# Hybrid attention block, 1 core: the first keys and queries of the differential stage loaded during linear attention, and the output projection's operand split one step ahead of its product

## The chip, the core and the metric

The kernel runs on one core of one Trainium2 chip. TensorE (PE) multiplies, VectorE (DVE), ScalarE (ACT) and GpSimd (POOL) do the elementwise work, SyncE (SP) issues most transfers. The metric is device microseconds of a whole execution, as the median of several runs; the kernel before took 4082.74 us (3 runs, 4078.76 to 4084.45).

## The reference, cut to what matters

Two layers (DEPTH 2) of a transformer block on 1024 latent and 256 context tokens of width 1024, in float32. Each layer projects the normalized tokens to heads, runs three kinds of attention, joins them, projects them out and adds a SwiGLU part:

```
pl = project_heads(modulate(h_lat, ...) @ w_in[layer], ...)
gla_lat = gla_output(ol_f + ol_b, pl['go'], gla_norm_g[layer])            # gated linear attention
diff_lat = diff_output(diff_latent(pl['dq'], dk_all, dv_all, lam), ...)   # p0 - lam * p1 over all 1280 keys
swa_lat = swa_output(swa_latent(...))                                     # sliding window
y_lat = jnp.concatenate([gla_lat, diff_lat, swa_lat], axis=-1) @ w_out[layer]
h_lat_mid = post_norm(h_lat, y_lat, m_lat[2], ln_g[layer, 0], ln_b[layer, 0])
```

In layer 0 the context tokens go through the same steps; in layer 1 (the last) only the latent tokens are queries. Tokens lie in tiles of 128: 10 tiles in layer 0, 8 in layer 1.

## The kernel before

The stages run one after the other, each in a block of its own: every engine has its list of instructions, engines meet through semaphores, and a stage ends with a barrier of all engines and a clearing of its semaphores by POOL (`cleanup_on_exit`). A layer is: input norm and projection, `gated_linear_attention` (L756), `differential_attention` (L1767), `sliding_window_attention`, the attention norm with the output projection (`norm_tiles`, kind "attention"), then `swiglu`. The last two attention stages lie inside a shared context (L2540) whose buffers the sliding window uses and the differential stage already fills.

**Differential stage.** At its start SP loads the queries of the first tile (3 transfers of 128 KB, L1853), then the keys of heads 0 to 3 (3 transfers of 320 KB each, L1859), then the next tile's queries. ACT issues one transfer for the values (`vT`, 1280 KB, L1962). One step r is one head of one tile: `score(i, r, 0)` and `score(i, r, 1)` on PE (L1901), row maximum on DVE (L2047), exponential on ACT (L1971), weighting on POOL, transposes and the product with V on PE. After the scores of the first step PE also turns the values (L1892, copied by ACT, L1995), and waits for `v_in` there. The first tile pair of layer 0 is context, with 256 keys a step; in all others a step has 1280 keys. Step r of the first tile waits for `k_in[r % 4]`, step 4 for the second tile's queries.

**Linear attention.** SP loads `kq` of heads 0 and 1 at the start and of heads 2 and 3 as their buffers come free (L911), then waits for the two halves of the result to store them (L926).

**Output projection and attention norm.** Matrices are multiplied as float32 in three products of split operands (hi·hi, hi·lo, lo·hi; L125 to L127). Per tile u:

- SP loads `mix` (one buffer), the joined attention columns, when the tile before has been split (L334), and `hres`;
- ACT copies the high part `mhi` (L522), POOL subtracts to get the low part `mlo` (L563); both have two buffers;
- PE multiplies by `w_out`: 48 matmuls of 512 columns into `Y` (two buffers);
- DVE: gate (L459), residual (L462), statistics (L431, L433), L466, L469, statistics again, `nmu` (L444); ACT gives the two deviations (L507);
- ACT normalizes (L513), PE transposes 8 blocks (L413), ACT modulates (L527) and makes `uhi` (L535), POOL `ulo` (L568).

These are placed in a software pipeline: in step r an engine does the parts of tile r − lag. Before, the split and the product have lag 0, SUM is 1 (DVE's gate to second statistics), NEXT is 2 (normalize, transposes, store) and SPLIT is 3. Within a step PE has the product, then the transposes; ACT has normalize (NEXT), `mhi` (0), modulate (SPLIT), first deviation (SUM), `uhi` (SPLIT), second deviation (SUM); POOL has `mlo` (0), then `ulo` (SPLIT); SP has `mix` and `hres` (0), then the store (NEXT).

Of the kernel before, what the change touches and what calls it, by code (L numbers as in the profile page):

```python
# [22 lines left out]
P = 128  # L23
# [175 lines left out]
def norm_tiles(nc, t, res, kind, layer, tiles, last):  # L199
# [13 lines left out]
    with nc.cleanup_on_exit(), ExitStack() as ctx:  # L213
# [5 lines left out]
        SUM = 1  # L219
        NEXT = 2 if post else 1  # L220
# [163 lines left out]
        def _(pe):  # L384
            def step(i, r, live):
                if attn and live(0):
                    s = r % 2
                    pe.wait_ge(mix_lo, count(i, r))
                    wait_count(pe, gated, count(i, r) - 2)
                    first = first_tile(i, r)  # L390
                    order = [(k, half) for k in range(KT) for half in range(2)] if first else [(k, half) for half in range(2) for k in range(KT)]
                    for k, half in order:
                        if first:
                            pe.wait_ge(wo_lo, k + 1)
                        cols = slice(half * BANK, (half + 1) * BANK)
                        mm = product(pe, Y[:, s, cols], mhi[:, s, k, :], mlo[:, s, k, :],
                                             wohi[:, k, cols], wolo[:, k, cols], k == 0, k == KT - 1)
                    mm.then_inc(y_done, 1)
# [357 lines left out]
def gated_linear_attention(nc, t, res, layer):  # L756


    with nc.cleanup_on_exit(), ExitStack() as ctx:
# [133 lines left out]
        def _(sp):  # L893
# [25 lines left out]
            for h in range(2, H):  # L919
                sp.wait_ge(unit_done, made(("diagonal", h - 2)))  # L920
                sp.wait_ge(x_dve, x_count(h - 2, len(LEVELS) - 1))
                sp.wait_ge(x_pool, x_count(h - 2, len(LEVELS) - 1))
                keys_and_queries(h)
            for i in range(2):
# [842 lines left out]
def differential_attention(nc, t, res, layer, tiles):  # L1767
    with nc.cleanup_on_exit(), ExitStack() as ctx:
# [12 lines left out]
        ks = sb(nm + "k", [96, UN, T], F32R)  # L1781
        qs = sb(nm + "q", [96, 2, UN, P], F32R)
# [25 lines left out]
        k_in = [sem(f"k_in{h}") for h in range(H)]  # L1808
        q_in = [sem(f"q_in{s}") for s in range(2)]
# [38 lines left out]
        def _(sp):  # L1848
            heads = t["heads"]

            def queries(i, s):
                for j, part in enumerate((0, 0, 1)):
                    sp.dma_start(qs[32 * j:32 * j + 32, s, :, :].bitcast(F32),  # L1853
                                 heads[part, HEAD_DQ:HEAD_DQ + 2 * P, bass.ds(i * 2 * P + s * P, P)].rearrange("(a p) n -> p a n", p=32)).then_inc(q_in[s], 16)

            def keys(h):
                rows = slice(HEAD_DK + 64 * h, HEAD_DK + 64 * h + 64)
                for j, part in enumerate((0, 1, 0)):
                    sp.dma_start(ks[32 * j:32 * j + 32, 2 * h:2 * h + 2, :].bitcast(F32), heads[part, rows, 0:T].rearrange("(a p) n -> p a n", p=32)).then_inc(k_in[h], 16)  # L1859

            def body(i, first):
                for s in range(2):
                    if not first:
                        sp.wait_ge(scores, 2 * (done(i, s * H + H - 1) - UN))
                    queries(i, s)
                    if first and s == 0:
                        for h in range(H):
                            keys(h)
# [10 lines left out]
        def _(pe):  # L1879
# [16 lines left out]
            def score(i, r, c):  # L1896
                h = r % H
                wait_count(pe, exp_done, 2 * (done(i, r) - 1) + c - 1)
                for a, n in KEYCH[:1 if is_ctx(i) else 3]:
                    n = min(n, N_CTX) if is_ctx(i) else n  # L1900
                    mm = pe.matmul(SC[:, c, a:a + n], qs[:, r // H, 2 * h + c, :], ks[:, 2 * h + c, a:a + n], start=True, stop=True)  # L1901
# [609 lines left out]
def build(nc, t):  # L2511
    with ExitStack() as outer:
# [18 lines left out]
        for layer in range(LAYERS):  # L2531
# [7 lines left out]
            gated_linear_attention(nc, t, res, layer)  # L2539
            with nc.cleanup_on_exit(), ExitStack() as local:  # L2540
                res["local"] = local_buffers(nc, local, layer)
                differential_attention(nc, t, res, layer, tiles)
                sliding_window_attention(nc, t, res, layer, tiles)
# [102 lines left out]
```

## Time and profile before

| | us |
|---|---|
| median of 3 runs | 4082.74 (4078.76 to 4084.45) |
| the profiled execution | 4078.89 |
| its span | 4077.1 |
| differential stage, first transfer to first score, layer 0 | 714.36 to 729.43 |
| the same, layer 1 | 2799.60 to 2814.75 |
| attention norm's second product to its last, layer 0 | 1132.14 to 1259.98 |
| the same, layer 1 | 3186.60 to 3282.20 |

Times in rows are microseconds from the span's start. In a row of the timeline the first number is the start, the second the duration (of a merged group, from its first start to its last end), and the bracket gives how long the engine had idled before and what released it. PEld is the weight load of TensorE, and a name that ends in q, as SPq, is the queue of instructions that issues.

### The profile page before, as it was taken

To read this page: it belongs to the slowest core of one execution; us is meant where nothing else is said; L and a number is where in the kernel's file an instruction comes from. 1 tells how busy PE (TensorE), PEld (TensorE's weight loads), DVE (VectorE), ACT (ScalarE), POOL (GpSimd) and SP (SyncE) were. 2 spreads that over 40 slices of the span, in tenths; PEclk is the share of its full clock that TensorE was granted. 3 is DMA by queue.
4 is the path that set the end of the run, shared out by engine and by line. 5 is a ranking of instruction groups with operands and counts; after the bars stand their busy time and mean duration, and the time that the engine had idled before them with its cause. 6 is when DMAs were issued, how large, how long until landed. Compare 5 with 4: busy or idle time off the path is not lost. (4 is left out here: it accounts for less than half of the span.)

```text
span 4077.1 us, 54961 instructions
## 1 busy us (share of the span) xinstructions
PE 3544.4 (87%) x21518; PEld 2921.1 (72%) x21518; DVE 1624.5 (40%) x2566; ACT 1438.6 (35%) x2413; POOL 1673.0 (41%) x1108
## 2 busy tenths in 40 slices
PE   6799588688786999999999599596989879999997
PEld 2488487466565888888888487385665668888886
DVE  2103454585574222224433204464855622223324
ACT  2211265585443111113232311375854432222221
POOL 1211152592323444435555211243933345555553
PEclk8899799698998999999999799697989889999998
DMA  8422310332232222222333223312343433333332
GB/s 287 163 87 105 130 27 14 77 71 55 85 128 91 65 63 62 63 67 88 114 100 112 86 89 112 99 31 72 75 135 95 165 97 95 94 98 109 114 99 93
DMA packets 171082, 388.51 MB, mean 95 GB/s; under 512 B 14536, under 2 KB 75048, under 8 KB 170864
## 3 DMA queue, kind: packets, MB, share of 16 engines
q1 hardware_dynamic: 149184, 334.38, 26.7%
q10 hardware_dynamic: 19200, 44.63, 2.9%
q0 software_dynamic: 2480, 6.48, 0.6%
q8 instruction: 151, 2.47, 0.3%
q14 instruction: 67, 0.55, 0.0%
HBM read 319.41 MB, written 66.03 MB: 95 GB/s over the span
## 5 line engine op out<-in xcount | busy, mean ns | idle before, releaser
L2332 POOL TENSOR_TENSOR ffn_wlo<-ffn_raw,ffn_whi 128x1024 fp32r<-128x1024 f32 x264 | 644.7, 2449 | 678.2 <-ACT ffn_whi L2244 678.2
L2244 ACT CAST ffn_whi<-ffn_raw 128x1024 fp32r<-128x1024 f32 x264 | 272.6, 1049 | 878.9 <-PE ffn_acc L127 464.8
L2466 DVE TENSOR_TENSOR ffn_silu<-ffn_up,ffn_silu 128x256 f32<-128x256 f32 (+1 forms) x143 | 75.3, 527 | 946.6 <-PE ffn_up L127 937.3
L125 PE MATMUL ffn_gate<-second_uhi,ffn_whi 128*128 128x256 f32 (+1 forms) x1144 | 375.5, 328 | 43.0 <-POOL ffn_wlo L2332 34.3
L126 PE MATMUL ffn_gate<-second_ulo,ffn_whi 128*128 128x256 f32 (+1 forms) x1144 | 374.5, 327 | 0.0
L127 PE MATMUL ffn_gate<-second_uhi,ffn_wlo 128*128 128x256 f32 (+1 forms) x1144 | 374.1, 327 | 0.0
L125 PE MATMUL ffn_up<-second_uhi,ffn_whi 128*128 128x256 f32 (+1 forms) x1144 | 371.2, 324 | 0.9 <-POOL ffn_wlo L2332 0.9
L126 PE MATMUL ffn_up<-second_ulo,ffn_whi 128*128 128x256 f32 (+1 forms) x1144 | 370.9, 324 | 0.0
L127 PE MATMUL ffn_up<-second_uhi,ffn_wlo 128*128 128x256 f32 (+1 forms) x1144 | 370.5, 324 | 0.0
L2478 DVE TENSOR_TENSOR y<-ffn_acc,y 128x512 f32<-128x512 f32 x360 | 248.2, 691 | 257.3 <-PE ffn_acc L127 257.3
L125 PE MATMUL ffn_acc<-ffn_whi,ffn_hhi 128*128 128x512 f32 x792 | 313.9, 396 | 21.8 <-DVE y L2478 20.6
L126 PE MATMUL ffn_acc<-ffn_wlo,ffn_hhi 128*128 128x512 f32 x792 | 311.6, 393 | 0.0
L127 PE MATMUL ffn_acc<-ffn_whi,ffn_hlo 128*128 128x512 f32 x792 | 311.2, 393 | 0.0
L657 POOL TENSOR_TENSOR in_wlo<-in_raw,in_whi 128x1024 fp32r<-128x1024 f32 x42 | 100.3, 2390 | 453.1 <-ACT in_whi L681 453.1
L125 PEld LDWEIGHTS ffn_gate<-second_uhi,ffn_whi 128*128 128x128 f32 x1144 | 220.8, 193 | 64.4 <-POOL ffn_wlo L2332 35.1
L126 PEld LDWEIGHTS ffn_gate<-second_ulo,ffn_whi 128*128 128x128 f32 x1144 | 221.2, 193 | 19.1
L127 PEld LDWEIGHTS ffn_gate<-second_uhi,ffn_wlo 128*128 128x128 f32 x1144 | 221.0, 193 | 17.7
L125 PEld LDWEIGHTS ffn_up<-second_uhi,ffn_whi 128*128 128x128 f32 x1144 | 218.2, 191 | 18.9 <-POOL ffn_wlo L2332 1.5
L127 PEld LDWEIGHTS ffn_up<-second_uhi,ffn_wlo 128*128 128x128 f32 x1144 | 217.9, 191 | 17.4
L126 PEld LDWEIGHTS ffn_up<-second_ulo,ffn_whi 128*128 128x128 f32 x1144 | 218.0, 191 | 17.1
L2047 DVE TENSOR_SCALAR_CACHE_REDUCE diff_scores<-diff_scores 128x1280 f32<-128x1280 f32 (+1 forms) x144 | 196.7, 1383 | 65.8 <-PE diff_scores L1901 64.2
L1971 ACT ACTIVATE diff_e<-diff_scores,diff_negmax 128x1280 f32<-128x1280 f32 (+1 forms) x144 | 178.3, 1239 | 66.2 <-DVE diff_scores L2047 65.4
(279 smaller groups left out, 7993.0 us busy)
## 6 DMA issues: line engine op xcount, KB each, us to landing
ffn_raw<-w_ffn_dram SPq DMA_DIRECT2D x264, 512.0 KB, 3.6
in_raw<-w_in_dram SPq DMA_DIRECT2D x42, 512.0 KB, 3.6
norm_input_ada_w<-w_ada_dram SPq DMA_DIRECT2D x10, 2048.0 KB, 8.3
swa_ada_w<-w_ada_dram SPq DMA_DIRECT2D x8, 2048.0 KB
proj_scratch<-in_stage ACTq DMA_DIRECT2D x20, 640.0 KB, 2.9
ada_w<-w_ada_dram SPq DMA_DIRECT2D x6, 2048.0 KB
gla_kq<-proj_scratch SPq DMA_DIRECT2D x32, 320.0 KB
local_qhl<-heads_scratch SPq DMA_DIRECT2D x36, 256.0 KB
```

The costliest lines, as they stand in the source:

```text
L125: pe.matmul(out, st_hi, mv_hi, start=start, stop=False)
L126: pe.matmul(out, st_hi, mv_lo, start=False, stop=False)
L127: return pe.matmul(out, st_lo, mv_hi, start=False, stop=stop)
L657: pool.tensor_tensor(wlo[:, s, :, :], raw[:, s, :].rearrange("p (k n) -> p k n", k=KT), whi[:, s, :, :].bitcast(F32), ALU.subtract).then_i ...
L1971: act.activation(E[:, r % 4, c, 0:keys], SC[:, c, 0:keys], ACT.Exp, bias=ng[:, c:c + 1], scale=-1.0, accum_out=den[:, c, tile_of(i, r), r ...
L2047: dve.tensor_scalar(SC[:, c, 0:keys], SC[:, c, 0:keys], -scale, 3e38, ALU.mult, ALU.min, accum_out=ng[:, c:c + 1]).then_inc(neg_done, 1)
L2244: act.copy(whi[:, w % 3, :], raw[:, w % 2, :]).then_inc(w_hi, 1)
L2332: pool.tensor_tensor(wlo[:, w % 3, :], raw[:, w % 2, :], whi[:, w % 3, :].bitcast(F32), ALU.subtract).then_inc(w_ready, 1)
L2466: dve.tensor_tensor(sg[:, n % 2, 0:tn], UP[:, n % 2, 0:tn], sg[:, n % 2, 0:tn], ALU.mult).then_inc(mul_done, 1)
L2478: dve.tensor_tensor(Y[:, tt, cols], ACC[:, half, :], Y[:, tt, cols], ALU.add).then_inc(y_added, 1)
```

## The change

Three edits. `gated_linear_attention` gets the list of tiles; two new buffers (head 0's keys and the first tile's queries) are made in a context around all three attention stages, and SP loads them in linear attention after head 3's `kq` and ahead of the first store. The differential stage takes them in place of its own: its SP begins with head 1's keys. In `norm_tiles` the product of a tile gets a lag of its own, PROD = 1, with the split left at 0, so that SUM, NEXT and SPLIT are 2, 3 and 4 for this stage (for the input norm, NEXT stays 1).

```diff
-        SUM = 1
-        NEXT = 2 if post else 1
+        PROD = 1
+        SUM = 2
+        NEXT = 3 if post else 1
         SPLIT = NEXT + 1
...
-                if attn and live(0):
-                    s = r % 2
-                    pe.wait_ge(mix_lo, count(i, r))
-                    wait_count(pe, gated, count(i, r) - 2)
-                    first = first_tile(i, r)
+                if attn and live(PROD):
+                    u, s = r - PROD, (r - PROD) % 2
+                    pe.wait_ge(mix_lo, count(i, u))
+                    wait_count(pe, gated, count(i, u) - 2)
+                    first = first_tile(i, u)
...
+def early_buffers(nc, ctx, layer):
+    sb, _, sem = allocators(nc, ctx, f"early{layer}_")
+    nm = f"early{layer}_"
+    return {
+        "keys": sb(nm + "keys", [96, 2, T], F32R),
+        "queries": sb(nm + "queries", [96, 2 * DIFF_HEADS, P], F32R),
+        "k_in": sem("k_in"), "q_in": sem("q_in"),
+    }
+
+
+def load_differential_keys(sp, t, dst, h, done):
+    rows = slice(HEAD_DK + 64 * h, HEAD_DK + 64 * h + 64)
+    for j, part in enumerate((0, 1, 0)):
+        sp.dma_start(dst[32 * j:32 * j + 32, :, :].bitcast(F32), t["heads"][part, rows, 0:T].rearrange("(a p) n -> p a n", p=32)).then_inc(done, 16)
...
                 keys_and_queries(h)
+            load_differential_queries(sp, t, res["early"]["queries"], tiles[0] * P, res["early"]["q_in"])
+            load_differential_keys(sp, t, res["early"]["keys"], 0, res["early"]["k_in"])
             for i in range(2):
                 sp.wait_ge(dve_took, taken(("root", i)))
...
-                    queries(i, s)
-                    if first and s == 0:
-                        for h in range(H):
-                            keys(h)
+                    if not first or s:
+                        load_differential_queries(sp, t, qs[s], i * 2 * P + s * P, q_in[s])
+                    else:
+                        for h in range(1, H):
+                            load_differential_keys(sp, t, ks[:, 2 * h - 2:2 * h, :], h, k_in[h])
...
-            gated_linear_attention(nc, t, res, layer)
-            with nc.cleanup_on_exit(), ExitStack() as local:
...
+            with nc.cleanup_on_exit(), ExitStack() as early:
+                res["early"] = early_buffers(nc, early, layer)
+                gated_linear_attention(nc, t, res, layer, tiles)
+                with nc.cleanup_on_exit(), ExitStack() as local:
```

## Rows read from the trace of the kernel before

**Rows 1.** Waits of PE, layer 0's attention norm: total, times, longest.

```profile
PE norm_attention_y L125 <- POOL norm_attention_mlo L563: 17.2, 8, 2.9
```

**Rows 2.** Timeline of PE: product of tile 2, transposes of tile 0, product of tile 3.

```profile
1144.69 0.50 PE L125 MATMUL norm_attention_y<-norm_attention_wohi,norm_attention_mhi 128*128 128x512 f32 x1
...
1155.71 1.03 PE L413 MATMUL norm_attention_tr<-ident,norm_attention_x 128*128 128x128 f32 x8
1158.75 0.54 PE L125 MATMUL norm_attention_y<-norm_attention_wohi,norm_attention_mhi 128*128 128x512 f32 x1 [2.01 <-POOL norm_attention_mlo L563]
```

**Rows 3.** Timeline of ACT and of POOL, one tile of layer 0.

```profile
1243.56 1.03 ACT L522 CAST norm_attention_mhi<-norm_attention_mix 128x1024 fp32r<-128x1024 f32 x1
...
1244.67 2.34 POOL L563 TENSOR_TENSOR norm_attention_mlo<-norm_attention_mix,norm_attention_mhi 128x1024 fp32r<-128x1024 f32 x1 [5.78 <-ACT norm_attention_mhi L522]
```

**Rows 4.** Timeline of DVE: a tile of layer 0, then one of layer 1.

```profile
1243.61 1.23 DVE L459 TENSOR_TENSOR norm_attention_h<-norm_attention_y,norm_attention_gate 128x1024 f32<-128x1024 f32 x1 [1.23 <-PE norm_attention_y L127]
1244.97 3.12 DVE L462 SCALAR_TENSOR_TENSOR norm_attention_h<-norm_attention_hres,norm_attention_h 128x1024 f32<-128x1024 f32 x1
...
1251.21 3.50 DVE L469 SCALAR_TENSOR_TENSOR norm_attention_h<-norm_attention_h,norm_attention_rstd,norm_attention_lnb 128x1024 f32<-128x1024 f32 x1
...
1256.96 0.16 DVE L444 SCALAR_TENSOR_TENSOR norm_attention_nmu<-norm_attention_mv,norm_attention_rstd 128x1 f32<-128x1 f32 x1
...
3199.48 1.23 DVE L459 TENSOR_TENSOR norm_attention_h<-norm_attention_y,norm_attention_gate 128x1024 f32<-128x1024 f32 x1 [5.00 <-PE norm_attention_y L127]
...
3208.60 0.16 DVE L444 SCALAR_TENSOR_TENSOR norm_attention_nmu<-norm_attention_mv,norm_attention_rstd 128x1 f32<-128x1 f32 x1
```

**Rows 5.** Stretches from second product to last, both layers: busy times, PEclk, DMA share, GB/s.

```profile
1132.14:1259.98 127.84, 113.05 (x491) 91.85 (x492) 98.42 (x116) 50.53 (x98) 35.62 (x15) 0.95 0.30 103
3186.60:3282.20 95.60, 87.66 (x378) 71.47 (x379) 67.93 (x90) 36.47 (x72) 28.29 (x12) 0.93 0.31 105
```

**Rows 6.** Timeline, start of layer 0's differential stage: first transfers, scores of steps 0 to 4.

```profile
714.36 1.33 SPq L1853 DMA_DIRECT2D diff_q<-heads_scratch  x3
...
729.43 0.77 PE L1901 MATMUL diff_scores<-diff_k,diff_q 96*128 96x256 f32 x2 [20.64 <-DMA diff_k<-heads_scratch]
...
735.61 0.80 PE L1901 MATMUL diff_scores<-diff_k,diff_q 96*128 96x256 f32 x2 [0.46 <-ACT diff_V L1995]
...
742.41 0.80 PE L1901 MATMUL diff_scores<-diff_k,diff_q 96*128 96x256 f32 x2 [2.98 <-DMA diff_k<-heads_scratch]
...
744.23 0.29 PEld L1901 LDWEIGHTS diff_scores<-diff_k,diff_q 96*128 96x128 f32 x1 [1.00 <-DMA diff_q<-heads_scratch]
```

**Rows 7.** Timeline, start of layer 1's differential stage.

```profile
2799.60 1.60 SPq L1853 DMA_DIRECT2D diff_q<-heads_scratch  x3
...
2814.75 2.47 PE L1901 MATMUL diff_scores<-diff_k,diff_q 96*128 96x512 f32 x6 [20.43 <-DMA diff_k<-heads_scratch]
...
2817.02 1.91 PE L1892 MATMUL diff_tr<-ident,diff_vT 128*128 128x128 f32 x8
...
2821.27 2.97 PE L1892 MATMUL diff_tr<-ident,diff_vT 128*128 128x128 f32 x12 [2.34 <-ACT diff_V L1995]
...
2824.70 1.46 PE L1901 MATMUL diff_scores<-diff_k,diff_q 96*128 96x512 f32 x6 [0.46 <-ACT diff_V L1995]
```

**Rows 8.** DMA queues at 716:720, 726:728, 2807:2809: packets, MB, share of 16 engines.

```profile
q10 hardware_dynamic: 222, 1.14, 73.8%
...
q1 hardware_dynamic: 111, 0.44, 100.5%
...
q10 hardware_dynamic: 14, 0.04, 4.5%
```

**Rows 9.** Timeline of SP in linear attention, layer 0.

```profile
655.97 54.70 SPq L926 DMA_DIRECT2D mix_scratch<-gla_out  x2
```

**Rows 10.** Instructions of the shared context's end, L2540: duration, first and last start.

```profile
L2540 POOLq DRAIN  x4: 34/50/66, 1101.8 to 3158.1; - x4
L2540 POOLq EVENT_SEMAPHORE  x4: 17/17/17, 1102.1 to 3158.3; - x4
```

More of the change, by code:

```diff
@@ L752, in _, with load_differential_queries, gated_linear_attention @@
             rope(IN_TILES - 1, pairs, 0, 1)
-def gated_linear_attention(nc, t, res, layer):
+def early_buffers(nc, ctx, layer):
[10 more added lines that the diff above has]
+        sp.dma_start(dst[32 * j:32 * j + 32, :, :].bitcast(F32), t["heads"][part, rows, 0:T].rearrange("(a p) n -> p a n", p=32)).then_inc(done, 16)
+def load_differential_queries(sp, t, dst, column, done):
+    for j, part in enumerate((0, 0, 1)):
+        sp.dma_start(dst[32 * j:32 * j + 32, :, :].bitcast(F32),
+                     t["heads"][part, HEAD_DQ:HEAD_DQ + 2 * P, bass.ds(column, P)].rearrange("(a p) n -> p a n", p=32)).then_inc(done, 16)
+def gated_linear_attention(nc, t, res, layer, tiles):
     with nc.cleanup_on_exit(), ExitStack() as ctx:
@@ L1780, in differential_attention, with key_rows @@
         t0, tn = tiles[0] * P, len(tiles) * P
-        ks = sb(nm + "k", [96, UN, T], F32R)
-        qs = sb(nm + "q", [96, 2, UN, P], F32R)
+        ks = sb(nm + "k", [96, UN - 2, T], F32R)
+        early = res["early"]
+        qs = [early["queries"], sb(nm + "q", [96, UN, P], F32R)]
+        def key_rows(u):
+            return early["keys"][:, u, :] if u < 2 else ks[:, u - 2, :]
         vT = sb(nm + "vT", [P, 2, T])
@@ L1807, in differential_attention @@
         const_in, v_in = sem("const_in"), sem("v_in")
-        k_in = [sem(f"k_in{h}") for h in range(H)]
-        q_in = [sem(f"q_in{s}") for s in range(2)]
+        k_in = [early["k_in"]] + [sem(f"k_in{h}") for h in range(1, H)]
+        q_in = [early["q_in"], sem("q_in1")]
         lam, lam_exp = sem("lam"), sem("lam_exp")
@@ L1848, in _ @@
         def _(sp):
[L1849 to L1859, printed above, removed]
             def body(i, first):
@@ L1900, in score @@
                     n = min(n, N_CTX) if is_ctx(i) else n
-                    mm = pe.matmul(SC[:, c, a:a + n], qs[:, r // H, 2 * h + c, :], ks[:, 2 * h + c, a:a + n], start=True, stop=True)
+                    mm = pe.matmul(SC[:, c, a:a + n], qs[r // H][:, 2 * h + c, :], key_rows(2 * h + c)[:, a:a + n], start=True, stop=True)
                 mm.then_inc(scores, 1)
@@ L2538, in build @@
                     input_projection(nc, t, res, layer)
-            gated_linear_attention(nc, t, res, layer)
-            with nc.cleanup_on_exit(), ExitStack() as local:
-                res["local"] = local_buffers(nc, local, layer)
-                differential_attention(nc, t, res, layer, tiles)
-                sliding_window_attention(nc, t, res, layer, tiles)
+            with nc.cleanup_on_exit(), ExitStack() as early:
+                res["early"] = early_buffers(nc, early, layer)
+                gated_linear_attention(nc, t, res, layer, tiles)
+                with nc.cleanup_on_exit(), ExitStack() as local:
+                    res["local"] = local_buffers(nc, local, layer)
+                    differential_attention(nc, t, res, layer, tiles)
+                    sliding_window_attention(nc, t, res, layer, tiles)
             with ExitStack() as ctx:
```

## Prediction

> **What bounds the kernel now.** The change touches two short places in each of two layers, so I read stretches, not shares of the whole. For the output projection I took PE's waits first: in layer 0 PE waited 17.2 us in 8 pieces for `mlo`, the low part of the tile's operand that POOL makes [rows 1]. The timeline shows the place of each: the product of a tile runs 11.0 us at full rate (1144.69 to 1155.71), the 8 transposes 1.0 us, then PE stands for 2.0 us until `mlo` of the next tile is there [rows 2]. Why is the split late? Its ACT part `mhi` stands behind the normalize of two tiles earlier, and that one is behind DVE's whole chain. ACT's copy takes 1.03 us, POOL's subtraction 2.34 us [rows 3], and only then the product may begin. So there is a cycle: product, DVE's chain (13.5 us from 1243.61 to 1257.12), normalize, `mhi`, `mlo`, product of the tile after next [rows 4]. PE and DVE each wait for the other in it. Between the second product's start and the last one's end PE's matmul records cover 113.05 of 127.84 us in layer 0 and 87.66 of 95.60 in layer 1, at a mean granted clock of 0.95 and 0.93 [rows 5]: the stretch is near to, but not at, the rate of PE alone.
>
> For the differential stage I read the timeline from its first instruction. In layer 0 the first transfer is issued at 714.36 and the first score starts at 729.43, after 20.64 us of idle PE that a transfer of keys ended; step 1 follows at 735.61, released by ACT's copy of V; step 3 at 742.41 waits for keys again and step 4 at 744.23 for queries [rows 6]. In layer 1 it is 2799.60 and 2814.75, step 1 is at 2824.70, again behind the copies of V, and no later one waits for keys [rows 7]. So one head's keys cost (742.41 − 729.43)/3 = 4.33 us of transfer and the queries of a tile 1.8 us.
>
> **Part 1, the split a step ahead.** No instruction is added or removed; the product moves behind the split by one step. In the new order, in step s, ACT has normalize(s−3), `mhi`(s), modulate(s−4), the first deviation of tile s−2, `uhi`(s−4), the second deviation; POOL `mlo`(s), `ulo`(s−4); PE product(s−1), transposes(s−3). `mlo`(s−1) is then made while product(s−2) runs, and it is 11 us long against 1.0 + 2.3 us for the split, so PE's wait for `mlo` goes. What is late next? Each candidate in turn. `mhi`(s) now waits for product(s−2), whose buffer it overwrites, and modulate and the deviations stand behind it on ACT; `mhi` of 1.03 us is done before DVE has run its 1.2 + 1.2 + 1.7 us to the first statistics, so no deviation gets later once the pipeline is full. Only tile 0's does: `mhi`(2) has to land first (issued after `mlo`(1)), 2 to 3 us later on DVE, with PE busy on product(1) meanwhile. SP issues `mix`(s) after `mlo`(s−1), past the wait for tile s−3's sum and the store of tile s−4, both long over. PE's transposes need normalize(s−3), which DVE released about a product earlier. Gate (s−3) is needed before product(s−1) overwrites `Y`; it is over 10 us earlier. So PE should go product, transposes, product without a stop, at 11.02 + 1.0 = 12.0 us a tile, if DVE and POOL keep up.
>
> Do they? Two prices bound a tile on DVE. Undisturbed it is 9.3 us (3199.48 to 3208.76); disturbed it is 13.5 us, because L462 takes 3.12 us and L469 3.50 us against some 1.25 alone, each when POOL runs at the same time (`mlo` started at 1244.67, L462 at 1244.97) [rows 3, 4]. The low end is below PE's 12.0, the high end above. Which holds depends on where DVE stands: started right at the product's end, it meets `mlo`(s), since `mhi`(s) waits for the same product; it then ends 1.5 us late for the next tile, but as `mhi`(s+1) stands behind the normalize it has then finished L462 before `mlo` starts, runs in some 10 us (9.3 and part of an overlap) and catches up. Alternating between 13.5 and 10 gives 11.8, just under 12.0. So I take PE as the bound, and add 1.5 us once a layer 1 for a last tile that ends in a bad phase.
>
> The Trainium skill, page "SBUF — State Buffer", section "SBUF: two separate sides", says that VectorE and GpSimd share one pair of ports under an exclusive lock, and that the one that starts first holds it for a whole instruction. The trace agrees with its kind: 3.12 and 3.50 us are an own time and the rest of POOL's instruction [rows 4]. Read strictly it would let every tile cost VectorE its 13.5 us, which is the second case below; read by who starts first it gives the alternation above.
>
> The sum for layer 0: the stretch of rows 5 becomes a first product as now (1132.14 to 1144.69, 12.55 us, it starts slow), 8 products of 11.02 and 7 sets of transposes of 1.0, 107.7 us against 127.84: 20.1 us saved. That is more than the wait of [rows 1], since after each of several stands PE ran some matmuls at the lower of its two rates (the mean clock of 0.95 [rows 5]), and without stands that goes too. Layer 1: 12.8 (3186.60 to DVE's start at 3199.48) + 6 × 11.02 + 5 × 1.0 = 83.9 against 95.60, 11.7 saved, less 1.5: 10.2. The tail after the last product is the same chain as now. Together 30.3 us.
>
> **Part 2, keys and queries early.** Six issues move into linear attention on SP, behind head 3's `kq` and ahead of the wait for the first store at 655.97: the transfers of `kq` are long issued by then and SP only stands there, so six issues at some 0.45 us (3 in 1.33 us) are hidden [rows 6, 9]. If the cover were gone they would cost 2.7 us a layer. Their 1.4 MB run while linear attention loads nothing. What this uncovers: the first scores can run at the start of the stage, but PE then waits in the same step for the values to turn them, and step 1 waits for head 1's keys.
>
> Layer 0: the keys and queries taken off the queue were 4.33 + 1.8 = 6.1 us of its time, so step 4 comes at 738.1 in place of 744.23. The stage's start shows more than that: K0 took 15.1 us to land, where its own 4.33, 1.8 for queries and about 3 for the values (a share of 73.8% over 4 us [rows 8]) add to 9 and a latency; some of the rest goes with the short rows of the queries. Bounds 4.8 and 9.3; I take 7.0, nearer to the rows' own 6.1.
>
> Layer 1: step 1 is what counts, since behind it each step is paced by ACT and DVE. It comes after the values have landed, by 7.7 us now, of which 2.3 is PE's wait for an ACT that had scores to take first [rows 7]; ACT is free of those in the new order, so 5.4. When do the values land? Now between 2807 and 2809, their last 14 packets are seen there [rows 8]. But now the queue beside them carries small rows of queries, and in the new order it carries keys from the first moment. A packet of values costs 0.738 × 4 × 16 / 222 = 0.21 us of an engine, one of keys 1.005 × 2 × 16 / 111 = 0.29 [rows 8]; 255 of values, each with one of keys between, take 255 × 0.50 / 16 = 8.0 us, after about 2.5 us to the first packet: 2810.1, and step 1 at 2815.5 against 2824.70, 9.2 saved. Ends of the range: values as early as now (2808, 11.3 saved) and together with head 1's keys at 2812.9 (6.4 saved). I take 9.0.
>
> The Trainium skill, page "DMA: Bandwidth & Descriptors", section "Queues, rings and completion order", has each engine take turns between queues, a packet at a time. That would be the sharing that I assume; no row of before shows the values beside keys, and without it the values would be as early as now.
>
> **Part 3, what it adds.** One more context ends after the sliding window in each layer. The inner one's end, L2540, goes from POOL's drain at 1101.8 to its last semaphore at 1102.1, 0.3 to 0.5 us with the barrier [rows 10]: 2 × 0.5 = 1.0 us lost. Nothing covers it, all engines stand.
>
> **The sum.** 30.3 + 7.0 + 9.0 − 1.0 = 45.3 us. The profiled execution took 4078.89 us, which would become 4033.6. The median of the runs is 3.9 us above it, so I forecast 4037.
>
> **The rivals.**
>
> *PE is the bound and the early loads pay (the forecast), chance 0.72.* Own range: 4028 to 4050 us, from the low ends (25 + 4.8 + 6.4 − 1.0 = 35) to the high ends (31.8 + 9.3 + 11.3 − 0.6 = 52) and the 3 us by which runs differ.
>
> *VectorE with GpSimd becomes the bound, 0.13.* If each tile stays at 13.5 us, DVE goes from tile 1 (1144.7) to tile 9 in 8 × 13.5 = 108 us, to 1252.7 in place of 1260.0, 7.3 saved, and in layer 1 6 × 13.5 from 3199.5 to 3280.5 against 3282.3, 1.8 saved. With 15 from the rest that is 24 us: 4059. For it: 3.12 and 3.50 occur in most tiles of layer 0. Against: the tile of 9.3 [rows 4].
>
> *The early loads buy nothing, 0.08.* The values land so late beside the keys, or the keys' stream starts later for another reason, that step 1 and step 4 come as now. Then 30.3 − 1.0: 4053. Against it speaks that 6.1 us of transfers are gone from a stream that is full.
>
> *The deeper pipeline gives a step back, 0.04.* If fill or drain grows by one PE step of 12.0 us in each layer, 24 us go: 4061. I see no instruction that waits for a step's end as such, only for data.
>
> *Slower, 0.03.* The first deviation stands behind `mhi` and modulate on ACT. Were the transfer of `mix` late, DVE would stand for it in every tile. Tiles now come at about 14.4 us (127.84 less 12.55, over 8); at 14 such tiles and 15 us gained elsewhere, each would have to cost 1.7 us more than now, over 16.1, to lose 0.2% of the whole. Disturbed DVE at 13.5 with `mhi` and a modulate of 2.9 us in front would be there: about 4095. Against: `mix` needs one landing a tile and has 12 us.
>
> **How the numbers follow.** 0.2% is 8 us, about what a measurement of this kernel tells from no change. All cases but the last are faster by more; with a little for cases between, faster 0.95, same 0.03, slower 0.02. The range of 4028 to 4059 holds the forecast's own range, the case of the loads and part of VectorE's.
>
> **What would show it.** Right: PE waits for `mlo` only before tile 1, tiles 12.0 us apart, clock 1.0 in the stretch; first scores within a us of the stage's start; step 1 of layer 1 some 16 us after it; step 4 of layer 0 some 23. Wrong: PE waiting in front of transposes (for normalize) or of products (for the gate), DVE's L462 and L469 at 3 us in each tile, the turning of the values starting over 13 us after the stage's start, or an idle ACT in front of the first deviation.

## The result and the profile after

The changed kernel takes 4028.88 us (median of 4 runs, 4025.98 to 4033.49) against 4080.75 (4 runs, 4072.12 to 4084.45) of the kernel before run beside it: ratio 0.9877, 95% interval 0.9858 to 0.9896. The forecast was 4037, its range 4028 to 4059, so the result lies just inside the low end. As a difference, 45.7 us were forecast and 51.9 came; in a second measurement beside other kernels (changed_again, below) it was 44.9. The profiled execution took 4030.76 us, with a span of 4028.9 against 4077.1: 48.2 us less.

Where it went, read as the time from a stage's first instruction to the next stage's first:

| stage | before | after | |
|---|---|---|---|
| differential, layer 0 | 228.1 | 221.3 | −6.8 |
| attention norm, layer 0 | 182.1 | 160.3 | −21.8 |
| differential, layer 1 | 198.6 | 190.0 | −8.7 |
| attention norm, layer 1 | 148.1 | 133.4 | −14.8 |
| all else | | | +3.9 |

The four touched stages give 52.1 us. The +3.9 is a net of differences in both directions between two single executions, with only the added context's 0.7 us in it that can be named as a cost of the change. The parts are +3.0 in linear attention of layer 0 (248.2 to 251.2), +4.4 in swiglu of layer 0 with the input projection of layer 1 (1299.2 to 1303.6), −3.2 and −2.8 in linear attention and the sliding window of layer 1, +2.4 in the rest. In linear attention of layer 0 the 248.2 is the lowest of twelve profiles: all others show 250.7 to 254.1, and 250.7 is of a kernel without early loads. The 1303.6 is the highest of twelve (1299.2 to 1302.2 in the others), in stages that no edit touches.

**The output projection.** PE's one wait for `mlo` in layer 0, between the second product and the last tile's gate (it answers [rows 1]):

```profile
PE norm_attention_y L125 <- POOL norm_attention_mlo L564: 2.4, 1, 2.4
```

It is the one before tile 1's product; the 8 waits of 17.2 us are gone. The timeline of PE around two sets of transposes (answers [rows 2]; overlapping records, so a start is the thing to read):

```profile
1153.43 1.03 PE L414 MATMUL norm_attention_tr<-ident,norm_attention_x 128*128 128x128 f32 x8
1154.22 0.48 PE L125 MATMUL norm_attention_y<-norm_attention_wohi,norm_attention_mhi 128*128 128x512 f32 x1
...
1165.22 1.03 PE L414 MATMUL norm_attention_tr<-ident,norm_attention_x 128*128 128x128 f32 x8
```

Transposes follow 11.79 us apart, and the product starts 0.79 us after them with no wait in the bracket. The stretches from second product to last (answer [rows 5]):

```profile
1129.96:1236.20 106.24, 106.24 (x491) 88.42 (x492) 88.61 (x117) 50.77 (x99) 39.71 (x15) 0.98 0.42 124
3150.89:3233.48 82.59, 82.59 (x379) 68.65 (x380) 67.67 (x90) 37.66 (x73) 29.07 (x11) 0.98 0.38 121
```

PE is busy for all of the 106.24 us where it was for 113.05 of 127.84, and the granted clock went from 0.95 and 0.93 to 0.98. What the waits had cost beside themselves shows in two products of the kernel before, tile 3's (behind a wait of 2.01 us) and tile 4's (behind 0.95). The columns are the stretch, its length, busy times of PE, PEld and DVE for instructions on `Y` alone, granted clock, DMA share and GB/s:

```profile
1158.75:1171.53 12.78, 12.78 (x48) 10.11 (x48) 0.00 (x0) 0.87 0.36 123
1173.37:1184.54 11.17, 11.17 (x48) 8.92 (x48) 0.00 (x0) 1.00 0.41 142
```

Of the seven products behind tile 2's in that stretch three took 12.78 us at a granted clock of 0.87 and four 11.2 at 1.00; in the change all from tile 2 on take 11.0 to 11.2. So of the 21.6 us that the stretch of layer 0 lost, 14.8 are waits for `mlo`, 4.8 are the three slow products, and most of the remaining 2.0 is that a product now starts 0.79 us after the transposes.

DVE and POOL over two tiles of layer 0 (answer [rows 4]):

```profile
1165.52 1.22 DVE L460 TENSOR_TENSOR norm_attention_h<-norm_attention_y,norm_attention_gate 128x1024 f32<-128x1024 f32 x1 [1.74 <-PE norm_attention_y L127]
1166.78 3.31 DVE L463 SCALAR_TENSOR_TENSOR norm_attention_h<-norm_attention_hres,norm_attention_h 128x1024 f32<-128x1024 f32 x1
...
1173.19 3.39 DVE L470 SCALAR_TENSOR_TENSOR norm_attention_h<-norm_attention_h,norm_attention_rstd,norm_attention_lnb 128x1024 f32<-128x1024 f32 x1
...
1178.82 0.16 DVE L445 SCALAR_TENSOR_TENSOR norm_attention_nmu<-norm_attention_mv,norm_attention_rstd 128x1 f32<-128x1 f32 x1
1179.11 1.23 DVE L460 TENSOR_TENSOR norm_attention_h<-norm_attention_y,norm_attention_gate 128x1024 f32<-128x1024 f32 x1
1180.48 1.23 DVE L463 SCALAR_TENSOR_TENSOR norm_attention_h<-norm_attention_hres,norm_attention_h 128x1024 f32<-128x1024 f32 x1
...
1188.69 0.16 DVE L445 SCALAR_TENSOR_TENSOR norm_attention_nmu<-norm_attention_mv,norm_attention_rstd 128x1 f32<-128x1 f32 x1
```

```profile
1166.60 2.41 POOL L564 TENSOR_TENSOR norm_attention_mlo<-norm_attention_mix,norm_attention_mhi 128x1024 fp32r<-128x1024 f32 x1 [2.96 <-ACT norm_attention_mhi L523]
...
1181.36 2.60 POOL L564 TENSOR_TENSOR norm_attention_mlo<-norm_attention_mix,norm_attention_mhi 128x1024 fp32r<-128x1024 f32 x1 [5.85 <-ACT norm_attention_mhi L523]
```

The first tile takes 13.5 us, with `mlo` begun 0.18 us before L463; the second 9.7, with L463 (1180.48) ahead of `mlo` (1181.36). The late start of the second is made good, as the prediction had it. It is not a strict turn about, though: tiles 2 to 8 of layer 0 took 9.6, 13.5, 9.7, 9.6, 13.7, 9.6 and 11.4 us, 11.0 on average, so long tiles are rarer than the every second one of the prediction.

**The differential stage.** Its start in layer 0, from the first transfer on (answers [rows 6]):

```profile
718.83 4.31 SPq L770 DMA_DIRECT2D diff_k<-heads_scratch  x9
...
719.02 0.77 PE L1919 MATMUL diff_scores<-early_keys,early_queries 96*128 96x256 f32 x2 [5.79 <-PEq L782]
...
729.67 4.88 PE L1910 MATMUL diff_tr<-ident,diff_vT 128*128 128x128 f32 x20 [9.88 <-DMA diff_vT<-proj_scratch]
...
735.20 0.51 PE L1919 MATMUL diff_scores<-diff_k,early_queries 96*128 96x256 f32 x2 [0.65 <-ACT diff_V L2013]
...
740.07 0.80 PE L1919 MATMUL diff_scores<-diff_k,early_queries 96*128 96x256 f32 x2 [1.26 <-DMA diff_k<-heads_scratch]
...
741.89 0.29 PEld L1919 LDWEIGHTS diff_scores<-early_keys,diff_q 96*128 96x128 f32 x1 [1.00 <-DMA diff_q<-heads_scratch]
```

The first scores start 0.2 us after the stage's start. The wait for keys has become one for the values, at 10.8 us. Step 3 still waits for keys, step 4 for queries, 23.1 us after the stage's start where it was 29.9. The same in layer 1 (answers [rows 7]):

```profile
2776.99 4.39 SPq L770 DMA_DIRECT2D diff_k<-heads_scratch  x9
...
2777.19 2.47 PE L1919 MATMUL diff_scores<-early_keys,early_queries 96*128 96x512 f32 x6 [5.20 <-PEq L782]
...
2787.74 4.92 PE L1910 MATMUL diff_tr<-ident,diff_vT 128*128 128x128 f32 x20 [8.08 <-DMA diff_vT<-proj_scratch]
2789.05 1.72 ACT L2013 COPY diff_V<-diff_tr 128x512 f32<-128x512 f32 x3
...
2793.31 1.43 PE L1919 MATMUL diff_scores<-diff_k,early_queries 96*128 96x512 f32 x6 [0.65 <-ACT diff_V L2013]
```

Step 1 comes 16.3 us after the start, where it was 25.1. The queues while the values move, 2779.3 to 2787 (packets, MB, share of 16 engines; q10 has the values, q1 the keys, q0 POOL's constants):

```profile
q10 hardware_dynamic: 272, 1.31, 49.9%
q1 hardware_dynamic: 178, 0.73, 34.4%
q0 software_dynamic: 122, 0.13, 19.2%
```

All 272 packets of values lie between 2.4 and 9.9 us after the stage's start. In the kernel before all 272 started between 2801.0 and 2807.8, 1.4 to 8.2 us after it. The added issues on SP (answers [rows 9]), behind the last `kq` and 56 us ahead of the store:

```profile
598.56 1.57 SPq L775 DMA_DIRECT2D early_queries<-heads_scratch  x3
600.18 1.39 SPq L770 DMA_DIRECT2D early_keys<-heads_scratch  x3
657.53 57.61 SPq L951 DMA_DIRECT2D mix_scratch<-gla_out  x2
```

### The profile page after: what moved, and what is told of

It is laid out like the page before. It is cut to its first block and busy times, and to the rows that moved or that the text cites. A ratio compares the mean times of both kernels' runs of the same rounds, so it can differ in the third digit from the quotient of the medians.

```text
span 4028.9 us, 54991 instructions
## 1 busy us (share of the span) xinstructions
PE 3537.6 (88%) x21518; PEld 2917.4 (72%) x21518; DVE 1615.7 (40%) x2566; ACT 1438.8 (36%) x2413; POOL 1677.6 (42%) x1108
## 5 line engine op out<-in xcount | busy, mean ns | idle before, releaser
L126 PEld LDWEIGHTS ffn_up<-second_ulo,ffn_whi 128*128 128x128 f32 x1144 | 217.9, 190 | 17.2
L125 PE MATMUL in_acc<-first_uhi,in_whi 128*128 128x512 f32 (+1 forms) x504 | 179.8, 357 | 20.7 <-POOL in_wlo L658 20.7
```

What stands on the lines that cost most here:

```text
L125: pe.matmul(out, st_hi, mv_hi, start=start, stop=False)
L126: pe.matmul(out, st_hi, mv_lo, start=False, stop=False)
```

## The experiments

Ten kernels, in three groups that shared a chip and the runs of the kernel before (medians 4075.86 of 12 runs, 4079.23 of 13, 4078.03 of 13). Stage times are read as in the table above, each from one profile, and the four columns are in us.

| kernel | median | ratio (95%) | norm 0 | norm 1 | diff. 0 | diff. 1 |
|---|---|---|---|---|---|---|
| split_ahead_only | 4041.08 | 0.9912 (0.9897 to 0.9927) | 160.6 | 135.4 | 228.5 | 199.0 |
| early_loads_only | 4060.15 | 0.9967 (0.9954 to 0.9979) | 177.8 | 146.6 | 221.1 | 189.6 |
| changed_again | 4030.96 | 0.9882 (0.9868 to 0.9897) | 159.5 | 133.4 | 221.0 | 191.5 |
| values_before_keys | 4031.42 | 0.9882 (0.9867 to 0.9897) | 159.9 | 133.2 | 221.9 | 191.9 |
| short_product_after | 4002.69 | 0.9822 (0.9804 to 0.9839) | 144.1 | 122.7 | 221.7 | 190.0 |
| short_product_before | 4056.64 | 0.9944 (0.9923 to 0.9964) | 167.9 | 139.3 | 228.0 | 199.1 |
| four_more_contexts | 4081.07 | 1.0006 (0.9996 to 1.0015) | 181.5 | 147.4 | 228.1 | 196.7 |
| values_first_lambda_later | 4029.18 | 0.9876 (0.9859 to 0.9893) | 159.9 | 133.7 | 221.7 | 188.4 |
| lambda_later_only | 4028.66 | 0.9879 (0.9862 to 0.9896) | 160.4 | 134.3 | 221.1 | 189.9 |
| mlo_in_halves_before | 4084.44 | 1.0014 (1.0004 to 1.0023) | 189.2 | 147.6 | 228.4 | 198.6 |

**Each part alone.** split_ahead_only has PROD, SUM and NEXT as in the change and none of its loads:

```diff
-        SUM = 1
-        NEXT = 2 if post else 1
+        PROD = 1
+        SUM = 2
+        NEXT = 3 if post else 1
```

> Only the lag of the product is changed (PROD 1); the loads stay where they were before. Theory (PE is the bound of the stretch once the split is ahead): the attention norm shrinks by some 36 us in both layers together, as in the changed kernel (182 to 160 us and 148 to 133 us), the differential stages stay at 229 and 200 us, and the whole comes out 33 to 38 us below before, near 4045. Rival (the gain of the changed kernel came from the loads, or the two parts need each other): less than 25 us.

early_loads_only has the early buffers and loads, the context around them, and the product in the split's step as before.

> Only the early keys and queries and the context around the three stages are kept; the product has its old lag. Theory: step 4 of layer 0 starts some 23 us after the stage's first transfer (30 before), step 1 of layer 1 some 16.3 us (25.1 before), the attention norm stays at 182 and 148 us, each layer loses up to 0.5 us to the context's end: 12 to 16 us below before. Rival (the loads disturb linear attention, which was 2.9 us longer in layer 0 of the changed kernel): linear attention longer by 3 us or more again, and under 10 us gained.

> The changed kernel itself, beside the others on the same chip: 45 to 52 us below before. The sum of the two parts alone should come to the same within 5 us if they are independent.

Measured, in their medians: the split saves 34.8 us, the loads 15.7, and both together 44.9. Two expectations are missed by a little: 44.9 for 45 to 52, and the sum of the parts, 50.5, lies 5.6 above the whole, not within 5. Both are within the intervals (0.0015 of the ratio is 6 us on each). The columns are sharper: each part changes its own stages by the full amount, and the split leaves the differential stages alone. One row says how far a single profile of the kernel before can be trusted: with the norm code of before, early_loads_only needs 177.8 us in layer 0 where before needed 182.1. POOL held L462 for over 3 us in one tile there (3.06), in four in before.

**The order of the transfers.** values_before_keys is the changed kernel with the values' issue moved from ACT to the head of SP's list:

```diff
         def _(sp):
+            sp.dma_start(vT[:, :, :], t["proj"][T_DV * P:(T_DV + 2) * P, 0:T].rearrange("(i p) n -> p i n", p=P)).then_inc(v_in, 16)
...
         def _(act):
-            act.dma_start(vT[:, :, :], t["proj"][T_DV * P:(T_DV + 2) * P, 0:T].rearrange("(i p) n -> p i n", p=P)).then_inc(v_in, 16)
```

> The changed kernel, with the values' transfer issued by SP ahead of head 1's keys instead of by ACT beside them. Theory (the values land late since they share the engines with the keys): the values land some 6.5 us after the stage's start instead of 10.8, step 1 of layer 1 starts at about 12.3 us instead of 16.3, so 4 us less there; layer 0's step 4 stays near 23 us, since it waits for the whole stream: 4 us below the changed kernel. Rival (the time to the values is latency or issue, not sharing): values at 10 us or more again, no difference, or the keys come so much later that layer 1 loses.

The time is that of the change, yet the values did land earlier. The timeline of its layer 1 (POOL's four constants were issued from 2775.99 on):

```profile
2775.50 0.39 SPq L1878 DMA_DIRECT2D diff_vT<-proj_scratch  x1
...
2783.79 1.97 PE L1912 MATMUL diff_tr<-ident,diff_vT 128*128 128x128 f32 x8 [5.62 <-DMA diff_vT<-proj_scratch]
2786.91 0.29 DVE L2052 TENSOR_TENSOR diff_lprod<-diff_lamv 128x32 f32<-128x32 f32 x2 [6.77 <-DMA diff_block_mean<-block_mean_dram]
...
2787.56 0.20 ACT L2011 ACTIVATE diff_lexp<-diff_lsum 128x2 f32<-128x2 f32 x1 [5.96 <-DVE diff_lsum L2055]
2787.67 1.05 ACT L2014 COPY diff_V<-diff_tr 128x512 f32<-128x512 f32 x2
...
2791.72 2.50 PE L1921 MATMUL diff_scores<-diff_k,early_queries 96*128 96x512 f32 x6 [0.46 <-ACT diff_V L2014]
```

PE turns the first values 8.3 us after the start, not 10.8. But ACT, idle since 2781.6, copies only at 2787.67, right behind the exponential for lambda, which stands ahead of the copies in ACT's list and needs DVE, which needs the small constants, which land 11.4 us after the stage's start. A wait that had been covered took the place of the one removed, and step 1 came at 16.2 us as before. The layer 1 gain of 4 us that was expected is not there, and neither is the rival's late landing. That the exponential took the place of the values is a theory until it is moved:

```diff
                 if first_step(i, r):
-                    act.wait_ge(lam, 4)
-                    act.activation(lexp[:, :], lsum[:, :], ACT.Exp).then_inc(lam_exp, 1)
                     for g, (j, a, n) in enumerate(VG):
...
+                    act.wait_ge(lam, 4)
+                    act.activation(lexp[:, :], lsum[:, :], ACT.Exp).then_inc(lam_exp, 1)
```

> The changed kernel with two edits: SP issues the values' transfer ahead of the keys (as in values_before_keys), and ACT's exponential for lambda, which waits for DVE and through it for POOL's four small constant transfers (landed 12 us after the stage's start), stands behind the six copies of V and not ahead of them. In values_before_keys PE turned the first values 8.3 us after the stage's start, but ACT's first copy came only at 12.2, right behind that exponential, and step 1 at 16.2 as before. Theory A, the exponential took the place of the values as what step 1 waits for: copies now start about 0.6 us after the turning, step 1 in layer 1 comes 13 us after the start in place of 16.2, which is 3 us for layer 1. In layer 0 step 1 is earlier too, but step 2 waits for head 2's keys at 17.6 us and step 4 for queries, so 0 to 1 us there. Time: 3 to 4 us under the changed kernel, 4027. Rival B, head 1's keys, which now come behind 1.28 MB of values, end the wait for step 1: it comes at 15 us or later, gain 1 us or none, 4031.

Its layer 1:

```profile
2781.20 0.39 SPq L1878 DMA_DIRECT2D diff_vT<-proj_scratch  x1
...
2789.66 2.48 PE L1912 MATMUL diff_tr<-ident,diff_vT 128*128 128x128 f32 x10 [5.79 <-DMA diff_vT<-proj_scratch]
2790.82 0.59 ACT L2012 COPY diff_V<-diff_tr 128x512 f32<-128x512 f32 x1 [3.52 <-PE diff_tr L1912]
...
2795.25 2.50 PE L1921 MATMUL diff_scores<-diff_k,early_queries 96*128 96x512 f32 x6 [0.46 <-ACT diff_V L2012]
```

The copies now wait for PE alone and step 1 comes at 14.05 us, 2.3 earlier than in the change (the first copy came 1.16 us after the turning, where 0.6 was expected). In layer 0 it moved from 16.4 to 13.6 us, but step 3 (21.5) and step 4 (23.4), which wait for keys and queries, stayed where they were (21.2 and 23.1), so nothing came of it. Theory A holds with 2.3 us for its 3; in the whole it can't be told from the change (4029.18 against 4028.88 and 4030.96 on other chips, and against 4028.66 of lambda_later_only beside it).

> The changed kernel with ACT's exponential for lambda behind the copies of V, the values' transfer on ACT as in the change. There the values were turned at 10.75 us after the start of layer 1's stage and ACT's first copy came at 12.06, 0.1 us behind the exponential, where about 11.3 was possible by PE. Theory A: step 1 comes 0.7 us earlier (15.5 to 15.6 us after the start), time 4030, no difference that can be told from the changed kernel. Rival B, the values are what ends the wait and the exponential never stood in the way: step 1 at 16.3 as before, time the same. The reading is the first copy's start, not the time.

With the values where the change has them, the copy began 1.15 us after the turning in place of 1.31, and step 1 came at 16.33 us, as in the change (16.32): rival B. In the change itself the values end the wait, and the exponential delays the first copy by 0.2 us and step 1 by nothing.

**What bounds the product's stretch.** In both short_product kernels `product` leaves out the second of its three matmuls in the attention norm (the one with the low part of `w_out`), so that PE has 32 for 48 a tile and nobody else has less. (The two expectations call it the third, low part of the operand times high part of the weights; the edit leaves out the other one, which takes as much of PE's time.)

```diff
     pe.matmul(out, st_hi, mv_hi, start=start, stop=False)
+    if short:
+        return pe.matmul(out, st_lo, mv_hi, start=False, stop=stop)
     pe.matmul(out, st_hi, mv_lo, start=False, stop=False)
```

> The changed kernel, but the output projection leaves out the third of its three products (low part of the operand times high part of the weights), 32 matmuls a tile instead of 48, so a product takes 7.3 us instead of 11.0. Theory (PE is the bound, VectorE's chain is just under it, at about 11.8 us on the average of disturbed and undisturbed tiles): the tile time falls from 11.8 only to what VectorE needs, between 9.9 and 11.8, not to 8.3, and PE waits again. That is under 2 us a tile, at most 25 us over both layers. Rival (VectorE had much room): tiles of 8.3 us, 45 us less. Second rival (VectorE was the bound already): no change.

> The kernel before with the same third product left out. Theory (the bound before is a cycle over two tiles: product 11.0, VectorE's chain 13.5, normalize 1.2, copy 1.1, subtraction 2.4, together 29.2 us, 14.6 a tile): the cycle shrinks by 3.7 us for two tiles, so a tile goes from 14.4 to about 12.6, some 1.8 us less, 25 us over both layers. Rival (PE alone was the bound, its stands are side effects): 3.7 us less a tile, 52 us. Second rival (VectorE alone): no change.

DVE in short_product_after, one tile and the next one's gate:

```profile
1168.79 1.22 DVE L462 TENSOR_TENSOR norm_attention_h<-norm_attention_y,norm_attention_gate 128x1024 f32<-128x1024 f32 x1
1170.15 1.23 DVE L465 SCALAR_TENSOR_TENSOR norm_attention_h<-norm_attention_hres,norm_attention_h 128x1024 f32<-128x1024 f32 x1
...
1174.78 1.28 DVE L472 SCALAR_TENSOR_TENSOR norm_attention_h<-norm_attention_h,norm_attention_rstd,norm_attention_lnb 128x1024 f32<-128x1024 f32 x1
...
1178.42 1.22 DVE L462 TENSOR_TENSOR norm_attention_h<-norm_attention_y,norm_attention_gate 128x1024 f32<-128x1024 f32 x1
```

With a third of the product gone a tile still takes 9.7 us (five tiles from 1139.85 to 1188.33), with DVE busy for 43.6 of 48.5 and going from one tile to the next gate without a wait: DVE's chain is the bound, and not one L465 of that stretch is held. So the worst case of the rival, DVE at 13.5 in each tile, doesn't arise even where DVE does bound: once it runs without a stop, `mlo` (at 1151.85) falls beside its statistics (two at 1151.99, 1.29 us together), which it doesn't hinder, and only the end of it beside L469 (L466 in before), which takes 1.6 to 1.7 us for 1.28. The expectation was a little too high for the tile (9.9 to 11.8) and too low for the gain: the two norm stages are 26.9 us shorter than in the change, where at most 25 was expected. The change left DVE 11.8 − 9.7 = 2.1 us of slack a tile against a chain that isn't held; with the held tiles that it does have, the average of 11.0 leaves 0.8.

In short_product_before each product is some 3.7 us shorter at the full clock, but tiles come 13.0 us apart (gates 1133.62 to 1250.86, nine steps) in place of 14.5 by the same reading, and PE waits for `mlo` up to 7.5 us in layer 0. In the medians 22.6 us came, where the cycle was to give 25 and PE as the bound 52. So the kernel before was paced by the cycle and not by PE.

**VectorE and GpSimd.**

```diff
-                    pool.tensor_tensor(mlo[:, s, :, :], mix[:, 0, :, :], mhi[:, s, :, :].bitcast(F32), ALU.subtract).then_inc(mix_lo, 1)
+                    for a in (0, KT // 2):
+                        k = slice(a, a + KT // 2)
+                        last = pool.tensor_tensor(mlo[:, s, k, :], mix[:, 0, k, :], mhi[:, s, k, :].bitcast(F32), ALU.subtract)
+                    last.then_inc(mix_lo, 1)
```

> The kernel before with POOL's subtraction for mlo cut into two instructions of 128x512 each, nothing else. It asks how VectorE and GpSimd hinder each other in the attention norm. Theory A, one holds the path for a whole instruction: L462 can now be held only for what is left of one half, so it takes 1.25 + at most 1.2 = 2.5 us in place of 3.12, and the second half of mlo then stands for VectorE's instruction in turn, so mlo ends up to 1.2 us later; the norm stage of layer 0 then changes by little, between -10 and +10 us. Rival B, both run at once at a lower rate: L462 and L469 keep 3.1 and 3.5 us wherever both halves follow each other, mlo's two halves take 2.4 together, the stage stays at 182.

POOL and DVE of this kernel at one tile:

```profile
1253.58 2.72 POOL L565 TENSOR_TENSOR norm_attention_mlo<-norm_attention_mix,norm_attention_mhi 128x512 fp32r<-128x512 f32 x2 [5.79 <-ACT norm_attention_mhi L522]
```

```profile
1252.73 1.23 DVE L462 SCALAR_TENSOR_TENSOR norm_attention_h<-norm_attention_hres,norm_attention_h 128x1024 f32<-128x1024 f32 x1
```

L462 took 1.23 us in all but four tiles of both layers, and 2.2 at most, where the kernel before has 3.07 to 3.21 in four of ten tiles of layer 0. In turn two of ten pairs of halves in layer 0 and four of eight in layer 1 took 3.5 us, where the others took 2.5 to 2.9. L469 still takes up to 3.51 us: it meets POOL's `ulo`, which was left whole. That is theory A. But the stage of layer 0 took 189.2 us, not 182.1 (layer 1 147.6, not 148.1), and the whole is 0.14% slower (0.04 to 0.23). PE now waits for `mlo` fewer times but longer, five times and 19.5 us in layer 0 where it was eight and 17.2, up to 4.2 us at a time; and behind each of the four waits from tile 3 on the product is slow, as tile 5's is here and tile 6's, without a wait, is not:

```profile
1194.89:1208.81 13.92, 13.92 (x48) 10.93 (x48) 0.00 (x0) 0.79 0.37 123
1209.44:1220.59 11.15, 11.14 (x48) 8.92 (x48) 0.71 (x1) 1.00 0.35 108
```

Four products of 13.9 us cost 11 us over the 11.2 of a product at full clock, where before three of 12.8 cost 4.8. So most of the 7 us is the clock and not the wait. Freeing DVE gained nothing while the cycle went through the very instruction that gave way.

**The context.**

```diff
-            with nc.cleanup_on_exit(), ExitStack() as local:
+            with nc.cleanup_on_exit(), nc.cleanup_on_exit(), nc.cleanup_on_exit(), nc.cleanup_on_exit(), nc.cleanup_on_exit(), ExitStack() as local:
+                for n in range(4):
+                    nc.alloc_semaphore(f"spare{layer}_{n}")
```

> The kernel before with four more nested contexts ending after the sliding window in each layer, each with a clearing of semaphores and a barrier; one semaphore more is cleared for each, no other work. Theory (0.3 to 0.5 us each): 8 ends cost 2.4 to 4 us in all, seen as a later start of the attention norm after the last store. Rival (they overlap with the landing of the last store or cost next to nothing): no time between the last store's landing and the norm's first instruction is added.

The last issue of the sliding window and the next stage's first instruction, in this kernel:

```profile
1101.75 1.27 ACTq L1677 DMA_DIRECT2D mix_scratch<-swa_oT  x2
1107.86 0.10 POOL L545 MEMSET norm_attention_eps<- 128x1 f32 x1 [15.65 <-POOLq L2540]
```

From the issue's end it is 4.84 us, against 3.41 in the kernel before: 0.36 us a context, and 0.33 in layer 1 (4.66 against 3.33). That is the theory, with 2.8 us for all eight, which the medians (1.8 us more, interval −2 to +6) can't tell from nothing. The change's one context shows 3.75 and 3.72, so 0.34 and 0.39.

## Why the prediction was right

**Part 1, the split a step ahead: forecast 30.3 us, 34.6 in the stretches.** That of layer 0 went from 127.84 us to 106.24 (forecast 20.1, came 21.6), that of layer 1 from 95.6 to 82.6 (forecast 10.2, came 13.0). The mechanism is the one forecast: one wait for `mlo` left, PE without a stop, the clock that the waits had cost given back, DVE between 13.5 and 9.7 us. Tile 0's late deviation is there too: DVE waited 2.4 us for it in layer 0 and 3.3 in layer 1 (forecast 2 to 3), while PE was on the next product. The term that was mis-sized is the period: I added 1.0 us of transposes to 11.02 of product, but the next product starts 0.79 us after them, and the period is 11.79, not 12.02. Over 7 and 5 periods that is 1.6 and 1.2 us, most of the error. The 1.5 us that I set aside for a last tile of layer 1 in a bad phase did not come. The stage of layer 1 was another 1.7 us shorter ahead of its second product; profiles of the same code spread by 2 us (133.2 to 135.4), so I claim nothing for it.

**Part 2, the early loads: forecast 7.0 + 9.0, came 6.8 + 8.8** by the steps named (step 4 from 29.87 to 23.06 us after the start, step 1 from 25.1 to 16.3), and 6.8 + 8.7 by the stages. The values were turned 10.75 us after the start where I had them land at 10.5, and from there to step 1 it was 5.6 us where I had 5.4. This closeness is partly luck. In layer 0 the 7.0 was chosen between 4.8 and 9.3. In layer 1 the sum put one packet of keys between any two of 255 values packets; the trace has 272 packets of values with 178 on the keys' queue and 122 of the constants beside them. Their 7.5 us from 2.4 to 9.9 us come near the forecast's 8.0 from 2.5 on, but not by that count; the 2.5 stood in no row of before, where the first packet of values came at 1.4. They landed 1.7 us later than before, of which 1.0 is the later first packet. What is shown is that the order matters: issued ahead of the keys, the values are turned 8.0 to 8.5 us after the start in both layers. As that also puts them on another queue, where packets move from 1.0 us on, it doesn't tell how much of the difference is sharing. The Trainium skill, page "DMA: Bandwidth & Descriptors", section "Queues, rings and completion order", has an engine take turns between queues, a packet at a time; this trace shows the queues side by side but not that the turns were one for one.

The cost of the six issues is nothing, as forecast: they end 56 us ahead of the store in layer 0 and 45 in layer 1.

**Part 3, the context: forecast −1.0 us, came −0.7** (0.34 + 0.39).

**The rivals.** VectorE as the bound fell by the profile after (PE without a stop) and, in its worst form, by short_product_after; it would give at least 9.7 us a tile and not 13.5. It was nearer than the clean result shows, though: 2.1 us of slack a tile with nothing held, 0.8 on average. The prediction also read the held L462 as the case in most tiles of layer 0; it is four of ten at over 3 us, while L469 is held in eight. The Trainium skill, page "SBUF — State Buffer", section "SBUF: two separate sides", has the two engines under an exclusive lock that the one that starts first holds for a whole instruction. The halves agree (2.2 us at most for 3.2), and so does the order of starts at 1166.60 and 1180.48; the strict reading that prices every tile at the held duration did not come true. Early loads that buy nothing: early_loads_only saves 15.7 us. A step more of fill or drain: from the last gate to the stage's end it is 24.2 us in layer 1 before and after. Slower: from tile 1 of layer 0 on DVE waited for a deviation for 0.4 us at most, as before; transposes of the full pipeline kept to 11.77 to 11.79 us.

**The total.** For the profiled execution the sum gave 4033.6, and 4030.76 came. Part 1 gave 4.3 us more than forecast, the norm stages another 2.0 outside the stretches, part 2 lost 0.5 and part 3 gained 0.3; against that stand 3.2 us in untouched stages, the net of the differences listed under the table of stages. That the sum came within 3 us is partly luck. The other 3.9 us of the forecast of 4037 were the distance of the median from that profile. Measured again, the median of before lay 1.9 above its profile, and that of after 1.9 below its own.

**What stays open.** Whether the values could be early too was not tried. Why stages of one and the same code differ by 3 to 4 us from one profile to another was not followed to its start: for the norm of before in layer 0 it shows as more or fewer tiles with L462 held, for linear attention nothing is known. Why a product behind one wait is slow and behind another of much the same length is not (2.57 and 2.86 us in before) isn't shown either.

## What to carry to other kernels

When three engines pass a tile around in one step, look for the cycle in which each waits for the other, and cut it by making the operand a step early: the gain is the wait and the clock that the waits cost, and the new period is read from the starts of instructions, not from the sum of their durations. When a transfer is taken off the head of a full queue, price what the stage waits for next with its new neighbours, and then look one further: behind the values stood a small constant that nobody had waited for. Relieving the engine that looks slow gained nothing here, since the relief delayed an operand on the cycle.

## What was not expected of the hardware

Four small constants, issued by POOL 0.5 to 3 us after the stage's start beside full queues, were usable at 11.3 us in layer 1 (DVE's first use at 2788.29, the stage's start at 2776.99) and, with the values in the same queue as the keys, at 10.9 to 13.0 in both layers.

That the two engines hinder each other is a matter of when they start: with DVE bound (short_product_after), its L462, L465 and L472, each of 1024 columns, took 1.22 to 1.29 us for five tiles in a row, and only L469 a little more (1.58 to 1.67), with POOL busy for 24.6 of the 48.5 us.

A wait of PE can cost more than its length: behind stands of 2.0 to 2.7 us three products ran at a granted clock of 0.87 (12.8 us for 11.2), and behind each of three of 4.15 us, in the kernel with the halves, one ran at 0.79 (13.9).
